# A two-block decoder layer in float32: attention scores from queries' high and low parts stacked on 128 partitions, moved by GpSimd's transfers, and another order in the drain of the heads

## What is computed

```python
def first_block(x, ...):
    h = rmsnorm(x, pre_mix_g)
    q_a, k_a, v_a, q_b, k_b, v_b, f_b = split(h @ w_in)        # 1024, 128, 128, 1024, 1024, 1024, 16
    o_a = swa_sink_attention(q_a, k_a, v_a, sinks)             # s = q k^T / 8 - slope * dist, banded, softmax with a sink
    log_f = log_sigmoid(f_b + b_forget)
    o_b = forgetting_attention(q_b, k_b, v_b, log_f)           # s = q k^T / 8 + c[t] - c[s], c = cumsum(log_f)
    mix = concatenate([rmsnorm(o_a, grp_swa_g), rmsnorm(o_b, grp_fox_g)]) @ w_out
    x = x + rmsnorm(mix, post_mix_g)
    u = causal_dwconv(rmsnorm(x, pre_ffn_g) @ w_up, conv_w, conv_b)
    gate, val = split(u)
    return x + rmsnorm((gelu(gate) * val) @ w_down, post_ffn_g)
```

## Time and profile before

| | us |
|---|---|
| median of 3 runs | 1655.26 (1655.14 to 1655.6) |
| profiled execution | 1655.94, of which its span 1654.0 |
| groups 3 to 7 with heads 0 to 19 | about 72 to 212.7 |
| last group with heads 20 to 23 | 212.74 to 244.14 |
| drain | 244.14 to 287.17 |

### The profile page before, as it was taken

How to read it: one execution, slowest core, us unless ns; L and a number is a source line. 1 busy time by engine, 2 the same in 40 slices (tenths; PEclk the granted TensorE clock), 3 DMA queues, 4 the chain that set the end, 5 groups by cost and what they waited for, 6 DMA issues and landing times.

```text
span 1654.0 us, 28292 instructions
## 1 busy us (share of the span) xinstructions
PE 1629.1 (98%) x11082; PEld 1489.6 (90%) x11082; DVE 1031.5 (62%) x1479; ACT 866.6 (52%) x1251; POOL 19.2 (1%) x43
## 2 busy tenths in 40 slices
PE   9999999999999999999999999999999999999996
PEld 8999988889999999999998888888998888898895
DVE  5566665666777777666764444465666455776555
ACT  6454556555555555454454444354433795655455
POOL 3000000000000000000000000010000000000000
PEclk9999999999999999999999999999999999999999
DMA  8654542646666666666665665565656557655551
GB/s 263 176 157 137 156 129 90 203 142 193 196 193 190 188 185 188 192 200 203 193 216 181 198 204 184 183 183 153 188 170 178 153 155 242 188 173 176 181 184 64
DMA packets 155599, 294.88 MB, mean 178 GB/s; under 512 B 13460, under 2 KB 16200, under 8 KB 154872
## 3 DMA queue, kind: packets, MB, share of 16 engines
q1 hardware_dynamic: 154632, 289.76, 56.9%
q0 software_dynamic: 848, 3.90, 0.6%
q10 hardware_dynamic: 32, 0.01, 0.0%
HBM read 291.53 MB, written 2.10 MB: 178 GB/s over the span
## 4 chain that ended last, share of the span: by engine, by line
PE 94%; DVE 3%; ACT 2%; DMA 1%; issue 1%; ACTq 0%; SPq 0%; DVEq 0%
PE bank L1862 29%; PE bank L1863 29%; PE bank L1864 29%; DMA raw<-in_w_in 1%; PE upper L2020 1%; DVE w_lo L1067 1%; PE upper L2250 1%; PE upper L2037 0%; PE upper L2023 0%; ACT w_hi L537 0%; PE upper L2053 0%; PE upper L2052 0%; PE upper L2294 0%; DVE x_tok L1497 0%; PE upper L2051 0%
## 5 line engine op out<-in xcount | busy, mean ns | idle before, releaser
L1067 DVE TENSOR_TENSOR w_lo<-raw,w_hi 128x1024 fp32r<-128x1024 f32 (+2 forms) x548 | 655.4, 1209 | 487.4 <-ACT w_hi L537 483.2
L537 ACT ACTIVATE w_hi<-raw 128x1024 fp32r<-128x1024 f32 (+2 forms) x548 | 565.8, 1047 | 506.4 <-PE bank L1864 489.9
L1862 PE MATMUL bank<-hT_hi,w_hi 128*128 128x256 f32 x2176 | 605.8, 278 | 3.2 <-DVE hT_lo L1142 1.5
L1863 PE MATMUL bank<-hT_lo,w_hi 128*128 128x256 f32 x2176 | 602.1, 277 | 0.0
L1864 PE MATMUL bank<-hT_hi,w_lo 128*128 128x256 f32 x2176 | 602.0, 277 | 0.0
L1862 PEld LDWEIGHTS bank<-hT_hi,w_hi 128*128 128x128 f32 x2176 | 408.8, 188 | 5.0 <-issue 2.8
L1863 PEld LDWEIGHTS bank<-hT_lo,w_hi 128*128 128x128 f32 x2176 | 408.9, 188 | 0.0
L1864 PEld LDWEIGHTS bank<-hT_hi,w_lo 128*128 128x128 f32 x2176 | 408.9, 188 | 0.0
L1862 PE MATMUL bank<-w_hi,hT_hi 128*128 128x512 f32 (+1 forms) x640 | 249.4, 390 | 0.0
L1864 PE MATMUL bank<-w_hi,hT_lo 128*128 128x512 f32 (+1 forms) x640 | 246.2, 385 | 0.0
L1863 PE MATMUL bank<-w_lo,hT_hi 128*128 128x512 f32 (+1 forms) x640 | 245.9, 384 | 0.0
(11 more groups left out here) (397 smaller groups left out, 1261.6 us busy)
## 6 DMA issues: line engine op xcount, KB each, us to landing
raw<-in_w_in SPq DMA_DIRECT2D x180, 512.0 KB, 3.9
raw<-in_w_up SPq DMA_DIRECT2D x176, 512.0 KB, 4.4
raw<-in_w_down SPq DMA_DIRECT2D x80, 512.0 KB, 4.2
raw<-in_w_out SPq DMA_DIRECT2D x64, 512.0 KB, 4.3
raw<-in_w_xkv SPq DMA_DIRECT2D x16, 512.0 KB, 4.3
raw<-in_w_down SPq DMA_DIRECT2D x16, 256.0 KB, 3.1
raw<-in_w_xq SPq DMA_DIRECT2D x8, 512.0 KB, 3.7
raw<-in_w_xo SPq DMA_DIRECT2D x8, 512.0 KB, 3.7
```

The lines of the kernel that those rows point to most:

```text
L537: act.activation(w_hi[:, s, at:at + n], raw[:, s, 0:n], ACT.Copy).then_inc(hi_ready, 1)
L1067: dve.tensor_tensor(w_lo[:, s, at:at + n], raw[:, s, 0:n], w_hi[:, s, at:at + n].bitcast(F32), ALU.subtract).then_inc(lo_ready, 1)
L1862: pe.matmul(o, l_hi, r_hi, start=start, stop=False, skip_group_check=True)
L1863: pe.matmul(o, l_hi, r_lo, start=False, stop=False, skip_group_check=True)
```

## The change

Queries and keys are now split into high and low float32r parts. A group's 512 columns x 256 tokens are written by VectorE as float32 into one staging tile `t_lo` (`t_out`); ScalarE copies them to `t_hi`, VectorE subtracts in place (`t_halves`), one piece into the next group (`T_OF`). GpSimd then moves 64 partitions at a time by transfers: a head's queries end up in `qs` with the high part on one half of the partitions and the low part on the other, a head's keys in `k_hi` and `k_lo` with the same 64 rows twice. The product of `qs` with `k_hi` and `k_lo` gives all four partial products in two float32r matmuls. A query set is 4 transfers of 256 KB, a key set 8. The shared keys of the sliding-window heads are split straight from PSUM (`ka_hi` on ScalarE, `ka_lo` on VectorE).

`t_hi` and `t_lo` share memory with `sT_hi` and `sT_lo`, so ScalarE's out_phase waits for the last key set to have been moved. `sT_lo`, the output of w_out (`y_mix`), some small tiles and the gate's weights `fr_raw` have new places, and `fr_raw` is now loaded from GpSimd's queue at the start of group gla_qk.

In the last group ScalarE and VectorE no longer split pieces 0 to 2 of w_out_a; these stand in `SPLITS` behind heads 22, 24 and 25. out_phase's second half (chunks 4 to 7) stands behind head 24, the values' copy of the last group (`vb`) behind head 25. TensorE keeps its order, but waits for the sT halves only ahead of its first out-projection piece (behind head 25), where it waited ahead of head 24.

```diff
+T_OF = {0: 1, 2: 2, 3: 3, 4: 4, 5: 5}
-SPLITS = ({24: 3, 26: 4, 28: 5, 31: 6, 33: 7}, {24: 3, 26: 4, 28: 5, 32: 6, 34: 7})
+SPLITS = ({22: 0, 24: 1, 25: 2, 26: 3, 27: 4, 29: 5, 31: 6, 33: 7}, {22: 0, 24: 1, 25: 2, 26: 3, 27: 4, 29: 5, 32: 6, 34: 7})
...
-            sp.dma_start(fr_raw[:, :, :], w_in2[:, GLR:GLR + 16].rearrange("(k p) n -> p k n", p=P)).then_inc(fr_loaded, 16)
...
-            pool.memset(ka2[:, :, :, :], 0.0).then_inc(k_cleared, 1)
-            pool.memset(kbT[:, :, :, :], 0.0).then_inc(k_cleared, 1)
...
+            def move_queries(i, e, read):
+                pool.wait_ge(t_low, i + 1)
+                if read:
+                    pool.wait_ge(scores_done, read)
+                for a in range(2):
+                    pool.dma_start(by_parity(qs, e)[halves[a], :, a, :], t_hi[halves[a], :, :]).then_inc(moved[i], 16)
+                    pool.dma_start(by_parity(qs, e)[halves[1 - a], :, a, :], t_lo[halves[a], :, :]).then_inc(moved[i], 16)
+
+            def move_keys(i, e):
+                pool.wait_ge(t_low, i + 1)
+                for a in range(2):
+                    for rows in halves:
+                        pool.dma_start(by_parity(k_hi, e)[rows, :, a, :], t_hi[halves[a], :, :]).then_inc(moved[i], 16)
+                        pool.dma_start(by_parity(k_lo, e)[rows, :, a, :], t_lo[halves[a], :, :]).then_inc(moved[i], 16)
+
+            move_queries(0, 0, 0)
+            move_queries(1, 1, 0)
+            move_queries(2, 0, NH // 2)
+            move_keys(3, 0)
+            move_queries(4, 1, NH)
+            move_keys(5, 1)
...
+            pool.dma_start(fr_raw[:, :, :], A["w_in_2"][0][:, GLR:GLR + 16].rearrange("(k p) n -> p k n", p=P)).then_inc(fr_loaded, 16)
...
+            def t_halves(i):
+
+                act.wait_ge(banks_free, evacuated((0, 2, 4, 5, 6, 7)[i]))
+                act.activation(t_hi[:, :, :], t_lo[:, :, :].bitcast(F32), ACT.Copy).then_inc(t_high, 1)
...
             def out_phase(chunks):
 
                 at = GAIN_AT["grp"]
+                act.wait_ge(moved[5], 128)
...
-                if j % 2:
+                if j == 0 and n in T_OF:
+                    t_halves(T_OF[n])
+                if j % 2 and j > 0:
                     head(4 * n + j // 2)
-                elif n == 5 and j >= 4:
-                    out_phase(range(2 * j - 8, 2 * j - 4))
-
-            for n, g in enumerate(range(3, 9)):
+            for n, g in enumerate(range(3, 8)):
...
-            for i in range(24, 2 * NH + 3):
+            for j in range(5):
+                split(early - 8 + j + SLOTS - 1)
+                last_sides(j - 1, 5)
+            out_phase(range(4))
+            for i in range(22, 2 * NH + 3):
                 head(i)
+                if i == 24:
+                    out_phase(range(4, 8))
+                if i == 25:
+                    act.wait_ge(mm_done, early)
+                    first_values(GROUP["v_b"][1])
                 if i in SPLITS[0]:
                     split(early + SPLITS[0][i])
...
+            def t_out(i, g):
+
+                if i:
+                    dve.wait_ge(moved[i - 1], 128 if i - 1 in (3, 5) else 64)
+                for b in range(NB):
+                    dve.tensor_tensor(t_lo[:, 2 * b:2 * b + 2, :].bitcast(F32), out_of(g, b).rearrange("p (a n) -> p a n", n=S),
+                                      x_row[:, :].unsqueeze(1).broadcast_to([P, 2, S]), ALU.mult).then_inc(banks_free, 1)
...
+                    q = qs[:, h, b * P:(b + 1) * P]
                     if i < NH:
-                        ins = pe.matmul(o[:, lo:hi], qaT[:, h // 2, b * P:(b + 1) * P], ka2[:, h // 8, h % 2, 0:n],
-                                        start=True, stop=True)
+                        pe.matmul(o[:, lo:hi], q, ka_hi[:, h // 8, 0:n], start=True, stop=False)
+                        ins = pe.matmul(o[:, lo:hi], q, ka_lo[:, h // 8, 0:n], start=False, stop=True)
                     else:
-                        pe.matmul(o[:, lo:hi], qbT[:, h // 2, b * P:(b + 1) * P], kbT[:, h // 2, h % 2, 0:n],
-                                  start=True, stop=False)
-
+                        pe.matmul(o[:, lo:hi], q, k_hi[:, h, 0:n], start=True, stop=False)
+                        pe.matmul(o[:, lo:hi], q, k_lo[:, h, 0:n], start=False, stop=False)
                         ins = pe.matmul(o[:, lo:hi], eye2[:, h:h + 1].broadcast_to([P, P]), cT2[:, 0:n], start=False, stop=True)
...
-            pe.wait_ge(loT_done, KC + 8)
-            pe.wait_ge(banks_free, evacuated(READER[1] - 1))
             early = 0
             for i in range(24, 2 * NH + 3):
                 head(i)
                 for _ in range(EARLY.get(i, 0)):
+                    if early == 0:
+                        pe.wait_ge(loT_done, KC + 8)
+                    if early == 4:
+                        pe.wait_ge(banks_free, evacuated(READER[1] - 1))
                     out_piece(GROUP["w_out_a"][early // 4], early % 4, 0)
```

125 lines of the change are left out of this document (70 added, 55 removed).

## The result

The changed kernel takes 1666.4 us (median of 4 runs, 1665.51 to 1667.57), the kernel before 1655.2 beside it: ratio 1.0062, interval 1.005 to 1.0075. It is slower by about 11 us, where I had forecast 1655.2 and a range up to 1663.5. The profiled execution spans 1664.9 us, 10.9 more than before.

A forecast was written before the change was run, and what follows sets the result against it. TensorE, 98% busy, was taken as the bound, with VectorE and ScalarE taking over in the drain. Scores -4.2, last group and drain +3.6, last transfer +0.5 gave -0.1 us: 1655.2, range 1650.5 to 1663.5.

The forecast's parts named there:

- What bounds the kernel: Whole kernel: TensorE busy 98% of the span; an edit pays only by shortening its list or changing where it waits.
- scores: Attention heads on TensorE: two float32r products each save 0.21 us a head, 6.7 us over all 32.
- moved work: Work moved onto VectorE, ScalarE and GpSimd costs nothing, covered by waits for TensorE; without cover 7.2 us.
- rival C: Attention scores: float32r products take as long as two passes, so the 4.2 us go: 1659.4; chance 0.06.
- The term -4.2: Twenty heads where TensorE is saturated: 0.21 us less each, 4.2 us, all on the path.
- The last transfer: Sixth key set, ScalarE's first sT_hi: starts 222.0, lands 233.0 or 236.0, reader can wait until 235.5; costs 0.5 us.
- Rival B: ScalarE's first sT_hi: last transfer at half rate, 5.5 us late, about 1 more through the clock: 1661.2; chance 0.27.
- The first five sets: GpSimd's transfers ahead of the last: at least 14 us before their reader, costed at nothing.
- The walk of the last group and the drain: Last group through drain: bound passes to VectorE and ScalarE, with more splits and sT halves between heads; 3.6 us longer.
- one fall of 0.9 us: Drain, out-projection piece 2: lower TensorE clock after a wait; 0.9 of the earlier 1.7 us reaches VectorE.
- The sum: Whole kernel: -4.2 + 3.6 + 0.5 = -0.1 us, set against the median 1655.26.
- alternative A: Drain: TensorE still sets it, all 32 heads pay, the gap and slow clock go: 10.8 us, 1644.5; chance 0.07.

The follow-up runs named there:

- old_order: The changed kernel with the kernel before's order of splits, out_phase and values' copy in the last group and drain: 1660.71 us, ratio 1.0025.
- own_place: The changed kernel with sT_hi in memory of its own, so ScalarE's out_phase no longer waits for the last key set: 1658.55 us, ratio 1.0012.
- old_order_own_place: The changed kernel with the kernel before's order and sT_hi in memory of its own, without the wait for the last key set: 1654.5 us, ratio 0.9986.
- half_copies: old_order_own_place with TensorE's sT wait moved to its first out-projection piece, GpSimd copying rows that stay on their half, transfers moving the rest: 1655.9 us, ratio 0.9997.

## Why the prediction was wrong

*What bounds the kernel, scores, moved work.* Right. TensorE, 98% busy; 0.21 us less a sliding-window head and 0.19 a forgetting one (201.05 to 202.75 against 203.49 to 205.38); rival C falls with them; no TensorE wait in after between 72 and 212 us. The four TENSOR_SCALARs began at 224.97, behind the last of the eight issues (223.90), so the rule of the Trainium skill's SBUF — State Buffer, "SBUF: two separate sides", on two-port VectorE operations wasn't put to the test there. fr_raw cost nothing: TensorE's product with it comes 10.9 us later than in before (1129.8 against 1118.9), and the span ends 10.9 later. ScalarE waited for raw once, 0.9 us, between 40 and 300 us in after, so weight loads pushed late did not decide it.

*The saving ahead of the last group.* The term -4.2 measured -2.6. The heads gave what the sum had; the sum took the distance between the products around them as fixed, and it grew by 3.4% in nine stretches.

*The last transfer.* The step that failed. I had 0.5 us from bounds of 11 and 14 us after its start; it took 18.6. Start and deadline held: TensorE reached the last group 2.6 us earlier than in the walk, and by that clock the 222.0 are 219.4 (issued from 219.68) and the 235.5 are 232.9 (the set landed at 238.28 and TensorE stood still for 5.36: 238.28 - 5.36 = 232.9). What was wrong is the time that eight transfers take. Its bounds came from the row of another kind of transfer, w_sgu's single one of 128 partitions that reads an input, and from a free bandwidth of 200 GB/s beside the weights, which these transfers couldn't use: 240 GB/s in all went through, 336 with 128 partitions. Rival B had the mechanism, the place and part of the price: 5.5 us late and 1 through the clock beyond the forecast's 0.9; the trace has 5.36 and 2.5, 8.2 us in all, the times 6.5 to 8.3. I gave it 0.27 because no row showed it. The Trainium skill's SBUF — State Buffer, "Door 1: The DMA port swizzle", has 196 against 328 GB/s at 1 MiB, a factor of 1.67. The trace agrees: by the sets here it is 18.6 us against at most 11.8, at least 1.6, and by the 2 us without weights 0.43 against 0.73 MB, 1.7. So "no row against a page's rule" should have weighed for the page.

*The first five sets.* "At least 14 us before their reader" was right and too loose: the first key set took 20.7 us (VectorE waited 0.28 at 181.06 in after), 24.0 in old_order. No such wait reached TensorE in after.

*The walk of the last group and the drain.* Right in kind: the bound passes to VectorE and ScalarE, the 2.5 us wait ahead of the first out-projection piece came as 2.28, and the waits for normalised heads 23 and 25, forecast as 1.4 and 3.8, as 2.12 and 2.17 (the first is put down to "issue", but VectorE's normalise ends 0.1 us before, at 263.45). Too small in size: +3.6 forecast against before's 74.43. own_place, which has this stretch without the late set, stands at +2.0 by its times after a gain of 2.6 ahead of it: 4.6. By its trace group and drain take 80.0 us (210.16 to 290.18), 5.6 more than before, where I had 78. The term that I argue is missing is the clock: I had one fall of 0.9 us, the windows of own_place show two:

```profile
248.00:252.00 4.00, 4.00 (x15) 3.23 (x14) 2.49 (x9) 2.37 (x7) 0.00 (x0) 0.57 0.40 131
...
264.00:268.00 4.00, 2.30 (x9) 2.14 (x10) 3.28 (x14) 2.72 (x12) 0.00 (x0) 0.63 0.38 133
268.00:272.00 4.00, 4.00 (x11) 3.13 (x10) 1.23 (x1) 1.26 (x3) 0.00 (x0) 0.51 0.07 22
```

(1 - 0.57), (1 - 0.63) and (1 - 0.51) x 4 us are 5.2 us in all, part of which lies in waiting. How much of it reached the end wasn't measured, so it stays open how much of the missing 1 to 2 us is the clock's.

*The sum.* -4.2 + 3.6 + 0.5 = -0.1 stands against -2.6 + 5.9 + 8.2 = 11.5 in the trace of after (8.2 from the late set, and the 5.9 left of the way from -2.6 to +11.5, where own_place has 5.6); all three terms erred to the same side. My alternative A (TensorE still sets the drain) is refuted by own_place, slower than before with no set late, and by old_order_own_place: even in before's order TensorE's lead of 3 us is used up by waits in the drain.

The version that beats both is old_order_own_place: new scores, before's order, no wait of sT_hi for the keys; 0.9986 of before, 12 to 13 us under after.

## What to carry to other kernels

A buffer that shares memory with the source of a transfer gives its writer a wait for that transfer; here other memory for 8 KB a partition was worth 6.5 to 8.3 us. Price a move between partitions by a transfer of its own shape; if the trace has none, take the slow figure as the forecast and the fast one as the rival. Where TensorE is full but the stage behind it is set by a chain of two other engines, a saving on TensorE ends at that stage, and an operation put among the chain's steps can cost more than its length (a split 3.0 us between two heads of before, of which VectorE's part is 1.2), and more where TensorE's clock falls behind the wait.

## What the runs showed of the hardware

- Eight transfers of 64 partitions x 4 KB, 2.1 MB in all, took 18.6 to 24.0 us beside weight loads; four of 128 partitions at most 11.8 us. In 2 us without weights they moved 0.43 and 0.73 MB. Packets four times as long changed nothing.
- GpSimd copies 64 partitions x 1024 float32 in 1.04 us when nothing holds them up; beside such copies two subtractions of VectorE took 4.04 us instead of 2.36 and four TENSOR_SCALARs 2.57 instead of 1.68, and one copy 2.03 (half_copies):

```profile
222.15 1.04 POOL L533 CAST k_hi<-t_hi 64x1024 fp32r<-64x1024 f32 x1
```

- A stream of products with 256 columns has two distances, 0.1137 and 0.1177 us, at the same granted clock; which one follows a head changed with one more product in the head (one trace).
- After standing still for 5.4 us TensorE ran at its lower level from 240.86 to about 246.5 (windows of 0.50 and 0.68), which cost it 2.5 us; it fell to windows of 0.50 to 0.73 after two of its three waits of 2.1 to 2.3.
